# Low parts of the first layer's front and gating projection formed by VectorE alone, with its other work reordered

## The reference

```
cond = silu(c)
mod = cond @ ada_w[0] + ada_b[0];  shift, scale, gate = split(mod, 3)
h = x * (1 + scale) + shift
u, v, z_a, x_b, z_b = split(h @ w_in)                    # 5 x 1024 columns
a = u * (W_s @ layer_norm(v) + b) * silu(z_a)            # per block of 128 tokens, 4 heads
b = ((pooled(x_b) @ pool_w + pool_b) * pool_scale) * silu(z_b)
y = concat(a, b) @ w_out
```

## Time and profile before

| | us |
|---|---|
| median of three runs | 1807.3 |
| lowest, highest | 1805.82, 1808.15 |
| the profiled execution | 1807.12 |
| its span in the profile | 1805.3 |
| TensorE busy | 1752.1 (97%) |
| VectorE busy | 1123.6 (62%) |
| ScalarE busy | 826.3 (46%) |
| GpSimd busy | 836.3 (46%) |

### The profile page before, as it was taken

The page is one execution under the profiler, slowest core; times in us unless marked ns, Lnnn a source line. Parts: engine busy times, 40 slices in busy tenths (PEclk is TensorE's granted clock), DMA queues, the critical chain, the costliest instruction groups (busy, mean ns, idle before and its releaser), DMA issues.

```text
span 1805.3 us, 29747 instructions
## 1 busy us (share of the span) xinstructions
PE 1752.1 (97%) x10544; PEld 1531.2 (85%) x10544; DVE 1123.6 (62%) x1924; ACT 826.3 (46%) x1397; POOL 836.3 (46%) x987
## 2 busy tenths in 40 slices
PE   8999999999999999999999999999999999999998
PEld 6778778878888878899899999888966799999886
DVE  7856646376666754888588777312668387776312
ACT  2423331365655552555365555323556465555322
POOL 3565566330101061766356656463423166666461
PEclk9999999999999999999999999999999999999999
DMA  9444555221211233134314344322311124343321
GB/s 368 155 145 129 163 177 202 94 78 39 67 47 52 70 129 117 47 98 135 117 47 117 94 115 118 127 93 94 112 69 47 47 71 117 93 116 93 129 94 70
DMA packets 195429, 193.73 MB, mean 107 GB/s; under 512 B 10896, under 2 KB 167312, under 8 KB 195344
## 3 DMA queue, kind: packets, MB, share of 16 engines
q1 hardware_dynamic: 195056, 192.45, 33.9%
q10 hardware_dynamic: 288, 0.16, 0.0%
HBM read 190.48 MB, written 2.10 MB: 107 GB/s over the span
## 4 chain that ended last, share of the span: by engine, by line
PE 63%; issue 14%; POOL 9%; DVE 8%; ACT 4%; DMA 2%; SPq 0%; POOLq 0%; DVEq 0%; ACTq 0%
PE PS L2219 20%; PE PS L2221 20%; PE PS L2220 20%; POOL w_low L747 3%; POOL slot_low L717 2%; POOL w_low L761 2%; DVE ada_raw L1401 1%; ACT w_high L872 1%; PE PS L2314 1%; POOL gate_sum_a L701 1%; POOL h_sum_low L707 1%; DMA w_raw<-in_o_w_out 0%; DVE masked L2161 0%; PE PS L2839 0%; DMA w_raw<-in_e_w_in 0%
## 5 line engine op out<-in xcount | busy, mean ns | idle before, releaser
L747 POOL TENSOR_TENSOR w_low<-w_raw,w_high 128x256 fp32r<-128x256 f32 x461 | 395.7, 893 | 410.9 <-ACT w_high L872 379.3
L717 POOL TENSOR_TENSOR slot_low<-w_raw,slot_high 128x256 fp32r<-128x256 f32 x400 | 318.1, 821 | 175.9 <-ACT slot_high L1211 173.3
L872 ACT ACTIVATE w_high<-w_raw 128x2048 fp32r<-128x2048 f32 (+2 forms) x86 | 157.5, 1831 | 307.9 <-PE PS L2221 296.7
L2219 PE MATMUL PS<-h_high,w_high 128*128 128x512 f32 (+1 forms) x688 | 248.2, 361 | 17.4 <-POOL w_low L747 7.1
L2220 PE MATMUL PS<-h_low,w_high 128*128 128x512 f32 (+1 forms) x688 | 241.8, 351 | 0.0
L2221 PE MATMUL PS<-h_high,w_low 128*128 128x512 f32 (+1 forms) x688 | 241.5, 351 | 0.0
L2219 PE MATMUL PS<-h_sum_high,slot_high 128*128 128x256 f32 x800 | 227.0, 284 | 3.7 <-DVE joined L1975 2.9
L2220 PE MATMUL PS<-h_sum_low,slot_high 128*128 128x256 f32 x800 | 226.4, 283 | 0.0
L2221 PE MATMUL PS<-h_sum_high,slot_low 128*128 128x256 f32 x800 | 226.4, 283 | 0.0
L2219 PE MATMUL PS<-h_high,slot_high 128*128 128x256 f32 x600 | 170.1, 284 | 1.9 <-ACT PS L1225 1.9
L2220 PE MATMUL PS<-h_low,slot_high 128*128 128x256 f32 x600 | 169.8, 283 | 0.0
(11 more groups left out here) (369 smaller groups left out, 4020.3 us busy)
## 6 DMA issues: line engine op xcount, KB each, us to landing
w_raw<-in_f_gate_up SPq DMA_DIRECT2D x88, 512.0 KB, 4.9
w_raw<-in_f_down SPq DMA_DIRECT2D x40, 512.0 KB, 4.1
w_raw<-in_e_w_in SPq DMA_DIRECT2D x32, 512.0 KB, 5.5
gains<-in_ada_t SPq DMA_DIRECT2D x16, 1024.0 KB, 5.0
w_raw<-in_a_w_in SPq DMA_DIRECT2D x24, 512.0 KB, 4.9
w_raw<-in_o_w_in SPq DMA_DIRECT2D x20, 512.0 KB, 4.6
ada_raw<-in_ada_t SPq DMA_DIRECT2D x16, 512.0 KB, 11.7
w_raw<-in_e_w_out SPq DMA_DIRECT2D x16, 512.0 KB, 4.5
```

The source lines that it names most:

```text
L717: ins = nc.gpsimd.tensor_tensor(slotL[j][:, piece], src[:, piece], slotH[j][:, piece].bitcast(F32), ALU.subtract)
L747: ins = nc.gpsimd.tensor_tensor(WL[s][:, piece], raw[s][:, piece], WH[s][:, piece].bitcast(F32), ALU.subtract)
L872: nact(WH[s][:, 0:n], raw[s][:, 0:n], ACT.Copy).then_inc(w_high[s], 1)
L2219: mm(dst, lh, rh, start=first, stop=False, skip_group_check=True)
```

## The change

GpSimd no longer works in stages 1 to 3. Low parts of both weight halves of the x_b loop, of all ten front chunks and of all eight zu chunks are formed by VectorE, in one instruction each. In detail:

- In the x_b loop from the second row on, ScalarE forms h twice: rounded, and in full float32 into `h_tmp`. It cuts the weights before that. For rows 1 to 3 the ada loads signal a semaphore of their own (`step_ada`), and the dots wait for that instead of the row's whole data. The small additions to `vec` come behind the first dots.
- VectorE's front list is written anew: the low parts of the chunks stand between pooled rows and dots. The sum of wT is copied out after the low part of the second v chunk; the first pool gate comes after the spatial gate.
- In zu the low part of chunk f+2 stands in round f, and the dots move from the start of the round to its end.
- SyncE's list keeps its order but for one load: `ada_load(4)` comes after the pool weights, not before the last two v chunks. ScalarE takes the high part of a z_b stage's next chunk ahead of silu, and loads the silu table before the pool gates' high parts (a dummy instruction on one column).
- Elsewhere three semaphores are merged into one counter (`k2_step`), with the same waits.

The diff, cut to these stages:

```diff
@@ -523,8 +527,8 @@
             first_x(0)
             first_weights(0)
             for kt in range(1, K):
-                first_ada(kt, 0, step_full[kt])
-                first_ada(kt, 1, step_full[kt])
+                first_ada(kt, 0, step_ada.get(kt, step_full[kt]))
+                first_ada(kt, 1, step_ada.get(kt, step_full[kt]))
                 first_x(kt)
                 first_weights(kt)
             sp.dma_start(bs_bc, a["gmlp_bs"].broadcast_to((P, a["gmlp_bs"].shape[1]))).then_inc(aux_in, 16)
...
@@ -556,15 +560,14 @@
             load_v(0)
             ada_load(3)
             load_v(1)
-            ada_load(4)
             load_v(2)
             load_v(3)
             pool_w = a["pool_w"].rearrange("g (k p) e -> p (g k) e", p=P)
             for half in range(2):
                 front(POOL_AT + half, [(raw[half][:, j * 512:(j + 1) * 512].rearrange("p (k e) -> p k e", e=256),
                                         pool_w[:, 4 * half + 2 * j:4 * half + 2 * j + 2, :]) for j in range(2)])
-            sp.wait_ge(xb_dve, K)
-            sp.wait_ge(xb_pool, K)
+            ada_load(4)
+            sp.wait_ge(xb_low, 2 * K)
             sp.dma_start(x[:, :, :], a["x"].rearrange("(t p) d -> p t d", p=P)).then_inc(x_in, 16)
             for c in range(8):
                 load_zu(c)
...
                 with pool.Fori(1, v.B.pairs) as i:
                     for s in range(2):
                         chunk(i, s)
-
-            for kt in range(K):
-                s, c = xb_slot(kt)
-                half = slice(c + HALF_D, c + D)
-                pool.wait_ge(xb_high, 2 * kt + 2)
...
-                if name == "front":
-                    for c in range(2 * pairs):
-                        if c != ZB_AT:
-                            low(c // 2, c % 2, FRONT_SIZE[c])
...
+                if name in ("front", "zu"):
...
             for kt in range(K):
-                act.wait_ge(*((step_full[kt], 80) if kt else (first_rows, 16)))
+                scale, shift = mod[:, K + kt:K + kt + 1], mod[:, kt:kt + 1]
+                if kt:
+                    xb_weights(kt)
+                else:
+                    act.wait_ge(first_rows, 16)
                 act.wait_ge(mod_ready, kt + 1)
-                nact(hH[:, kt, :], xT[:, kt, :], ACT.Identity, scale=mod[:, K + kt:K + kt + 1], bias=mod[:, kt:kt + 1]).then_inc(hx_high, 1)
-                xb_weights(kt)
+                nact(hH[:, kt, :], xT[:, kt, :], ACT.Identity, scale=scale, bias=shift).then_inc(hx_high, 1)
+                if kt == 0:
+                    xb_weights(kt)
+                    continue
+                if kt >= 2:
+                    act.wait_ge(hx_low, kt - 1)
+                nact(h_tmp[kt % 2], xT[:, kt, :], ACT.Identity, scale=scale, bias=shift).then_inc(h_sum, 1)
             front_high(ZB_AT)
 
             def xb_out(f):
...
+                front_high(ZB_AT + 2 + q)
                 zb_gate(q)
-                front_high(ZB_AT + 2 + q)
             pooled_high(3)
             front_high(V_AT + 2)
             front_high(V_AT + 3)
...
-            zb_high(0)
-            zb_high(1)
             front_high(POOL_AT + 3)
-            for f in range(2, K):
+            nact(stat[:, 0, 7:8], eps[:, 0:1], ACT.Silu)
+            for f in range(K):
                 zb_high(f)
 
             def gated(name, highs, fn):
...
+                dve.wait_ge(*((first_scale, 16) if kt == 0 else (step_ada[kt], 32) if kt in step_ada else (step_full[kt], step_count(kt))))
...
+                    steps.link(ins)
                 dve.wait_ge(ada_first, kt + 1)
                 v.tensor_tensor(mod[:, kt:2 * K:K], mod[:, kt:2 * K:K], vec[:, kt:2 * K:K], ALU.add).then_inc(mod_ready, 1)
-                dve.wait_ge(mod_ready, kt + 1)
+                s, c = xb_slot(kt)
+
+                def weights_low():
+                    for j in range(2):
+                        of, to = slice(j * HALF_D, (j + 1) * HALF_D), slice(c + j * HALF_D, c + (j + 1) * HALF_D)
+                        dve.wait_ge(xb_high, 2 * kt + j + 1)
+                        v.tensor_tensor(WL[s][:, to], xb_raw[kt][:, of], WH[s][:, to].bitcast(F32), ALU.subtract).then_inc(xb_low, 1)
+
+                def rows_low():
+                    dve.wait_ge(h_sum, kt + 1)
+                    dve.wait_ge(hx_high, kt + 1)
+                    v.tensor_tensor(hL[:, kt, :], h_tmp[kt % 2], hH[:, kt, :].bitcast(F32), ALU.subtract).then_inc(hx_low, 1)
+
                 if kt == 0:
+                    dve.wait_ge(mod_ready, 1)
                     dve.wait_ge(first_rows, 16)
-                v.tensor_scalar(h_tmp[kt % 2], xT[:, kt, :], mod[:, K + kt:K + kt + 1], mod[:, kt:kt + 1], ALU.mult, ALU.add).then_inc(h_sum, 1)
-                dve.wait_ge(h_sum, kt + 1)
-                dve.wait_ge(hx_high, kt + 1)
-                v.tensor_tensor(hL[:, kt, :], h_tmp[kt % 2], hH[:, kt, :].bitcast(F32), ALU.subtract).then_inc(hx_low, 1)
-                s, c = xb_slot(kt)
-                dve.wait_ge(xb_high, 2 * kt + 1)
-                v.tensor_tensor(WL[s][:, c:c + HALF_D], xb_raw[kt][:, 0:HALF_D], WH[s][:, c:c + HALF_D].bitcast(F32),
-                                ALU.subtract).then_inc(xb_dve, 1)
+                    v.tensor_scalar(h_tmp[0], xT[:, 0, :], mod[:, K:K + 1], mod[:, 0:1], ALU.mult, ALU.add).then_inc(h_sum, 1)
+                    rows_low()
+                    weights_low()
+                else:
+                    weights_low()
+                    rows_low()
+                if kt in (1, 3):
+                    dve.wait_ge(xb_low, 2 * kt + 2)
+                    dve.sem_inc(raw_free[s], CREDIT)
 
             def ada_terms(pos):
 
...
                     dve.wait_ge(act_high, GATED["zb"] + f + 1)
                     v.tensor_tensor(mixL[:, f + K, :], buf[f % 2][:, :], mixH[:, f + K, :].bitcast(F32), ALU.subtract).then_inc(gate_low, 1)
 
+            def front_low(c):
+                split_low("front", c // 2, c % 2, FRONT_SIZE[c])
+
+            def zu_low(c):
+                split_low("zu", c // 2, c % 2)
+
+            front_low(ZB_AT)
             ada_terms(0)
-            dve.wait_ge(w_high[0], BASE["front"].split[0] + 1)
-            v.tensor_tensor(WL[0][:, 0:ZB_DVE], raw[0][:, 0:ZB_DVE], WH[0][:, 0:ZB_DVE].bitcast(F32), ALU.subtract).then_inc(front_dve, 1)
             pool_rows(0)
+            front_low(ZB_AT + 1)
             pool_rows(1)
-            ada_terms(1)
             pool_rows(2)
+            front_low(ZB_AT + 2)
             pool_rows(3)
             pooled_low(0)
+            ada_terms(1)
             rest_columns()
-            ada_terms(2)
+            front_low(ZB_AT + 3)
             pool_rows(4)
             pool_rows(5)
             pooled_low(1)
+            front_low(V_AT)
+            ada_terms(2)
+            pool_rows(6)
+            front_low(V_AT + 1)
             dve.wait_ge(sum_done, 1)
             v.tensor_copy(ws_sum, PS[:, 7, :].rearrange("p (h t) -> p h t", h=G_HEADS)).then_inc(ws_sums, 1)
-            pool_rows(6)
             pool_rows(7)
+            pooled_low(2)
+            front_low(V_AT + 2)
             ada_terms(3)
-            pooled_low(2)
             pooled_low(3)
+            front_low(V_AT + 3)
             gate_norm(0)
+            front_low(POOL_AT)
+            front_low(POOL_AT + 1)
             gate_norm(1)
+            zu_low(0)
             dve.wait_ge(aux_in, 16 * 2)
             dve.wait_ge(ws_sums, 1)
-            pool_gate(0)
             for f in range(K):
                 spatial(f)
+            zu_low(1)
             gate_spread(0, GATE_POS - 1)
-            for f in range(2, K, 2):
+            for f in range(0, K, 2):
                 pool_gate(f)
 
             for f in range(2 * BASE["zu"].pairs):
                 i, s = f // 2, f % 2
-                ada_terms(MOD_POS + f)
                 dve.wait_ge(sg_ready, SG["zu"] + f + 1)
                 v.tensor_tensor(buf[s][:, :], buf[s][:, :], PS[:, 2 * s + 1, :], ALU.mult).then_inc(pair_free[s], 1)
                 dve.wait_ge(pair_free[s], PF["zu"] + i + 1)
                 v.tensor_tensor(buf[s][:, :], buf[s][:, :], sv[:, f, :], ALU.mult).then_inc(prod_ready, 1)
+                if f + 2 < 2 * BASE["zu"].pairs:
+                    zu_low(f + 2)
                 dve.wait_ge(prod_ready, GATED["zu"] + f + 1)
                 dve.wait_ge(act_high, GATED["zu"] + f + 1)
                 v.tensor_tensor(mixL[:, f, :], buf[s][:, :], mixH[:, f, :].bitcast(F32), ALU.subtract).then_inc(gate_low, 1)
+                ada_terms(MOD_POS + f)
             gate_keep(0, 6)
 
             def split_tail(name):
```

More of the change, by code:

```diff
@@ L202 @@
 Z_DVE = 1024
-ZB_DVE = 1536
 def program(nc, a, out):
@@ L368, in program @@
         step_full = [sem(f"step_full{kt}") for kt in range(K)]
+        step_ada = {kt: sem(f"step_ada{kt}") for kt in (1, 2, 3)}
         first_scale, first_shift, first_rows, c_in = (sem(n) for n in ("first_scale", "first_shift", "first_rows", "c_in"))
```

(47 more changed lines are left out.)

30 lines of the change are left out of this document (15 added, 15 removed).

## The result

The changed kernel takes 1836.7 us (median of 4 runs, 1835.7 to 1837.4), the kernel before 1807.7 (1805.8 to 1809.2) beside it: ratio 1.0157, 95% interval 1.0145 to 1.0169. It is slower, as forecast, but by 29.0 us and not by 20, and the time lies 0.7 us above the range's upper end.

A forecast was written before the change was run, and what follows sets the result against it. TensorE, busy 97% of the first 275 us, was taken as the bound. Removed stops put it about 15 us ahead, then chained loads in zu and the output projection turned this into +20.4 on 1807.12: 1827, range 1812 to 1836.

The forecast's parts named there:

- What bounds it: First 275 us: TensorE busy 97%, so only its stops, 14.9 us before 250, can give time back.
- Part 1: x_b loop: VectorE's step falls to about 4.9 us, below TensorE's 5.46; the 1.33 stop goes, six steps save 2.4.
- Part 2: Gating, v, pool weights: stops of 2.60, 1.29 and 2.14 us go; a new ws_sum wait appears; v ends at 148.0.
- 2.7 lost: First v chunk: TensorE waits at 107.0 for the ws_sum copy, ready at 109.6; 0 to 4 us by the landing.
- Part 3: VectorE's chain into zu: the 3.71 stop and 1.7 of slow clock go; first round ends at 189.8.
- Part 4: In zu each round chains ada and chunk loads: 15.8 us against TensorE's 10.9; zu ends 278.5 instead of 271.3.
- Part 5: Output projection: its first chunks are chained the same way; the third is split about 315.2, before it began at 294.8.
- so the 20.4 us stay: From the output projection's third chunk on, dots and chunk loads have room again, leaving the loss at 20.4 us.
- Not slower: Rival in zu: the chain of loads never binds, zu runs 166.1 to 253.3, time 1789; chance 0.08.
- Chain weak: Rival in zu: both transfers keep full rate, rounds of 13.7 us, 2.8 lost a chunk, time 1815; chance 0.12.
- Worse in the front: Rival before zu: VectorE's strict list is late there too, moving everything behind by 3 to 10 us, 1836; chance 0.05.
- The rule: Skill's DMA section: semaphore waits hold the issuing sequencer before dispatch; its fit gives 6.8 us for two megabytes, about 1815.

The follow-up runs named there:

- e3: The changed kernel with VectorE's ws_sum copy put ahead of the second v chunk's low part instead of behind it: 1831.0 us.
- f5: The changed kernel with the gate dots first in each zu round and the ws_sum copy ahead of the second v chunk's low part: 1788.4 us.
- f8: The changed kernel with GpSimd forming all zu low parts and dots first in each round; x_b loop and front stay as changed: 1798.6 us.
- e1: The changed kernel with the gate dots back at the start of each zu round, VectorE keeping all low parts: 1793.5 us.
- e2: The changed kernel with only SyncE's list changed, each ada load in zu and eout one chunk's weight load later: 1795.0 us.
- e4: The kernel before with VectorE's two gate dots moved to the end of each zu round, GpSimd still forming every low part: 1835.2 us.
- e9: The changed kernel with half of each ada load left out from position 5 on, orders and waits kept: 1824.8 us.
- f7: The changed kernel with the gate dots one place earlier, ahead of the mixed low part, still behind the next weights' low part: 1827.4 us.

## Why the prediction was right in kind and short in size

*What bounds it, and Part 1.* Right. No stop behind the x_b loop's first matmul (0.22 is the longest); VectorE's steps there are 4.8 us (dots at 34.54, 39.31 and 44.08), under TensorE's 5.46. One step took 6.57, with 1.71 of waiting for its data, and held nothing up.

*Part 2.* The three stops went as said: without the copy's stop the sum has the pool weights at 145.3, and e3 has them at 145.0, f5 at 145.3. The step that failed first is "2.7 lost" for the ws_sum copy. The stop was 3.35, and behind it the clock was granted at 0.76 over 107 to 114, partly the 1.2 GHz level, which the sum had priced at nothing:

```profile
107.00:114.00 7.00, 3.65 (x9) 2.77 (x9) 6.35 (x7) 1.30 (x3) 0.00 (x0) 0.76 0.50 164
```

e3 gives the term's true size, 5.3 us at the pool weights and 5.7 in the time. They started at 150.3 and not at 148.0: +2.4 in the rounded ledger below, of which 0.65 is stop (the load was there at 105.4, forecast 104.8) and some 1.7 is clock: 0.24 of 7 us. f8, with this stop and the full clock, has them at 148.6.

*Part 3.* Right in order, 1.2 us short over eleven steps: mainly the 0.23 us of hand-over behind each low part (190.40 above). Round 0 ended at 193.4, forecast 189.8.

*Part 4.* Right. Rounds of 15.95 were forecast as 15.8, the one with the gate bias 18.2 as 17.3; from 193.4 to 275.4 it is 82.0 against 80.7, +1.3. Of the stops, 3 to 5 us by the forecast, two lie outside, 2.34 and 5.14. The terms hold one by one: pair of loads 8.47 (8.65), ScalarE to VectorE 1.95 (1.85), low part to mixed 2.5 (2.25), the rest 3.0 (3.05). e1, e2 and e4 show the mechanism, e9 that the pair's bytes are in it, f7 that what leaves the row shortens it.

*Part 5.* Right in place, short by 3.5; here is the second step that failed. From the last dots to TensorE's start on the output projection 18.7 were needed where 17.6 were forecast (pair of loads 8.3 against 7.6, hops), +1.1; the third chunk's start another +0.4 (321.6 against 315.2 in all). The sum ended there with "so the 20.4 us stay". They didn't: +2.0 came after it. 0.2 of this is a reading (before's third chunk starts at 294.63, not 294.8). The rest is the clock, again priced at nothing: from 321.59 to the projection's end TensorE has no stop at all, and 0.71 over 320 to 325 with 0.95 over 325 to 330 is 1.7 us lost. Windows of after, the first from the zu stage, the second behind that last stop:

```profile
224.00:229.00 5.00, 4.98 (x12) 3.91 (x13) 4.27 (x7) 0.00 (x0) 0.00 (x0) 0.50 0.15 15
```
```profile
320.00:325.00 5.00, 3.41 (x9) 2.71 (x10) 0.28 (x2) 1.57 (x1) 4.82 (x7) 0.71 0.68 228
```

In the zu stage the slow clock costs little, since the next stop swallows it (after 5.14 us of stop all of 224 to 229 is at 0.50, and the following stop is 2.34 in place of some 5). Where no next stop follows soon, after the v stage's and after the last one, it stays in the time.

Ledger of the profiled executions: forecast +20.4, measured +28.75 at VectorE's first instruction after the projection (375.32 against 346.57). The difference of 8.3 is 2.4 (copy and clock) + 1.2 (hops) + 1.3 (rounds) + 1.1 (pair ahead of the output) + 0.4 + 2.0 (after the third chunk); 8.4 by the rounded terms. So what failed is the sizes in the sum, not the mechanism. Of the 8.3 us, 3.4 are slow clock behind two stops, which the sum had at nothing. The other 4.9 are small terms taken too short: 0.65 the first stop, 1.2 hops, 1.3 the rounds (0.9 of it the one with the gate bias), 1.1 the pair ahead of the output projection, 0.4 and 0.2 at its third chunk. The first part of the clock is shown by e3 and by e1 against f8; the other terms are read from the trace and were not tested by themselves.

The range's upper end fails by its own terms as well. Pairs of loads of 10.2 in place of 8.65, in the seven places where the gate bias wasn't counted already, give at least 11 us more, so 1838 and not 1835. That the time lies outside by 0.7 us is partly luck: the four executions run from 1835.7, which is inside, to 1837.4, and a full clock behind the first stop, as f8 had it, is worth 1.8. The 8.3 us as a whole are not luck.

*The rivals.* "Not slower" at 1789 is what e1 (1793.5) and f5 (1788.4) show once the coupling is cut, so its size was right and its condition wasn't met. "Chain weak" needed rounds of 13.7 and fell at 15.95. "Worse in the front", 1836 and a chance of 0.05, gave the measured time and a part of the cause: the ws_sum wait lengthened and moved all that follows, by 2.4 us; the other 6 were spread over the chain.

*The rule.* By the fit of the Trainium skill (DMA: Bandwidth & Descriptors, "Anatomy of one DMA"), taken on another issuing queue, two megabytes take 6.8 us, an estimate, by which the sum would have been 1815. The pair took 8.47 here, and the trace's rows were the better guide. That a load stands in SyncE's list behind the wait ahead of it is what e2 shows: put ahead of that wait, it goes out at 175.36 and not at 193.82.

## What to carry to other kernels

A load queued behind a wait in the issuing engine's list is as late as that wait: before an instruction is moved, look up which load its semaphore releases, and what stands behind that load. Price a round as the whole loop that closes (consumer, issue, both transfers, each hand-over) and compare it with the pace of the engine that should bind; if it is longer, the excess comes once per round. Here either end of the coupling could be cut, and cutting both gave nothing more. Price a stop with the clock behind it: the same stop of 3.19 us cost 1.8 us more in one execution than in another.
